# Two transformer blocks on one core: the three post-norms, the norms behind them and the output worked in halves of the tokens

## The chip, the cores and the metric

One core of a Trainium2 chip runs the whole program in one launch. The metric is the device time of an execution in microseconds (us). The core has a matrix engine (PE, which multiplies a stationary 128x128 tile with a moving one and writes PSUM), a vector engine (DVE), an activation engine (ACT), a general engine (POOL), and SyncE (SP), which issues the DMAs here. Each engine runs its own list of instructions in the order written; they wait for each other on semaphores.

## The reference

512 tokens with 1024 channels go through two blocks, all in float32. The first is a gated mixer (a depthwise convolution, a gated delta rule with 8 heads in both directions), a gated feed-forward part, a gated per-layer input and a last norm. The second is a feed-forward part, a mixer (pooled windows and window attention with sinks), and a feed-forward part again; each of its three parts has a norm before and a norm after it. What bears on the change:

```python
def rms_norm(x, g):
    return x * lax.rsqrt(jnp.mean(x * x, axis=-1, keepdims=True) + NORM_EPS) * g

x = x + jax.nn.sigmoid(rms_norm(x, g_pl[i]) @ w_pl_gate[i]) * pl
x = rms_norm(x, g_final)

h = swiglu(rms_norm_2(x, ffn1_pre[l]), ffn1_w_gu[l], ffn1_w_down[l])
x = x + 0.5 * rms_norm_2(h, ffn1_post[l])
h = token_mixer(rms_norm_2(x, mix_pre[l]), ...)
x = x + rms_norm_2(h, mix_post[l])
h = swiglu(rms_norm_2(x, ffn2_pre[l]), ffn2_w_gu[l], ffn2_w_down[l])
x = x + 0.5 * rms_norm_2(h, ffn2_post[l])
```

Every norm takes the mean square over all 1024 channels of a token. Different tokens don't meet in it.

## The kernel before, in words

**Layout.** Activations lie with channels on the 128 partitions: `x` is 8 tiles of 128 channels by 512 tokens. A **unit** is one weight block of 128 output channels, loaded by SP into one of four slots `w_raw`. Each float32 operand is split into a high and a low part (`w_hi` by ACT at L1020, `w_lo` by DVE at L1446; `a_hi` by ACT at L1295, `a_lo` by DVE at L1471), so a unit of a projection from 1024 channels is 8 x 3 = 24 products of 128x512 at L571 (`products`). A down projection of a feed-forward part has 22 channel tiles, two units (66 products) for one output tile. All go to the two banks of `pg`, in turns; an `Outs` table names who evacuates each. `gemm` counts finished units, and `hi`/`lo` of unit n + 2 wait for unit n (`after`).

**Order of the work.** It is written out by hand, one list an engine. The stages of this study, by unit names: `pg` 0 to 7 (gate of the per-layer input), `fg1`/`fu1` and `fd1` (first feed-forward part of block two), `mk`, `mv`, `mq`, `mu` (mixer), `mo` 0 to 7 (its output), `fg2`/`fu2`, `fd2`, and then the output.

**A norm** (`square`, `adds`, `norm`, `root`, `recip`, `norm_out`). ACT squares each tile into one of two buffers `sq`, POOL adds them up in `acc` (L2073), PE sums over channels with one-column products against ones (L602, 16 passes, since a float32 product of PE is two), ACT takes the root (L1042), DVE the reciprocal (L1458), PE spreads it over the partitions (L609, 8 passes), and DVE copies it to `rstd` (L1462). A norm whose result only scales columns of a product is put in late: the next stage's products run on unscaled `x`, and their evacuation multiplies with `rstd`; `norm_out` sits 14 products (`NORM_AT`) into the second unit of that stage.

**The post-norms** can't be put in late, since their result is added to `x`. After `fd1`, `mo` and `fd2` the function `post` scales the kept output (`hb`, `hb2`) by `rstd`: the first four tiles (`PD`) on DVE at L1924, the other four on POOL at L2146. DVE adds each to `x` (L1928), ACT makes `a_hi` and the square of the new `x`, and DVE `a_lo`. After `pg` the last norm of block one takes its place: DVE multiplies `x` with gain and `rstd` (L1909). The first unit of the next stage waits for `a_lo`, tile by tile. After `fd2` SP stores each of the 8 tiles of `x`.

## Time and profile before

| what | us |
|---|---|
| median of 3 runs | 2404.41 |
| lowest, highest | 2402.77, 2405.77 |
| the profiled execution | 2404.79 |
| its span | 2402.9 |
| PE busy | 2230.9 |
| DVE busy | 1304.9 |
| ACT busy | 788.9 |
| POOL busy | 327.7 |

The span runs from the first to the last event of the core in the profile. Busy time of PE counts overlapping, pipelined products once, with ends that are modelled, so it doesn't say that PE works at its peak. The time of a stage is best read from starts of products. Numbers in the timeline are microseconds from the start of the span.

### The profile page before, as it was taken

What the parts mean: (1) busy time and instruction counts of PE and PEld (TensorE: products, weight loads), DVE (VectorE), ACT (ScalarE), POOL (GpSimd) and SP (SyncE); (2) the same over time, 40 slices, a digit from 0 to 9 for tenths busy, and PEclk for the clock granted to TensorE, in tenths of its full rate; (3) what the DMA queues carried; (4) which work ended last, traced back from release to release, by engine and by line L of the source; (5) the groups of instructions that cost most, each with busy time, mean ns of one, the idle gap of its engine ahead of it and who ended that gap; (6) DMA issues with size and microseconds to landing.
All of it is one profiled execution on the core that took longest, in us unless ns stands there. A gap on an engine that the chain in (4) does not pass through costs nothing.

```text
span 2402.9 us, 33875 instructions
## 1 busy us (share of the span) xinstructions
PE 2230.9 (93%) x13850; PEld 1832.4 (76%) x13850; DVE 1304.9 (54%) x1750; ACT 788.9 (33%) x1106; POOL 327.7 (14%) x228
## 2 busy tenths in 40 slices
PE   6999888899899999999999979999988897999996
PEld 4877777778787878888888768888876575888885
DVE  4578798887654446444443354444226835444423
ACT  4345222225433223333322333332223443323221
POOL 0100442130343310100000120000011212000001
PEclk8999899999899999999999979999997986999998
DMA  3232011112111123322232312223221111222321
GB/s 139 82 115 79 28 54 41 45 50 79 36 41 41 54 71 137 122 96 96 96 108 93 105 53 96 96 96 108 96 85 44 36 59 45 97 96 96 111 94 40
DMA packets 54901, 189.68 MB, mean 79 GB/s; under 512 B 6144, under 2 KB 6400, under 8 KB 54784
## 3 DMA queue, kind: packets, MB, share of 16 engines
q1 hardware_dynamic: 51904, 182.75, 22.6%
q10 hardware_dynamic: 2880, 5.24, 0.6%
q8 instruction: 89, 1.46, 0.3%
q14 instruction: 28, 0.23, 0.0%
HBM read 178.53 MB, written 9.44 MB: 78 GB/s over the span
## 4 chain that ended last, share of the span: by engine, by line
PE 77%; DVE 13%; issue 6%; ACT 2%; DMA 1%; SPq 0%; POOL 0%; DVEq 0%; ACTq 0%; POOLq 0%
PE pg L571 65%; PE pC L746 3%; PE pB L602 2%; DVE cpad L1490 2%; DVE w_lo L1446 1%; DVE x L1928 1%; DVE a_lo L1471 1%; PE pB L746 1%; PE pC L609 1%; PE pB L609 1%; DVE oT L1490 1%; DVE sacc L1600 1%; DVE cacc L1490 1%; ACT w_hi L1020 1%; DVE hb L1924 1%
## 5 line engine op out<-in xcount | busy, mean ns | idle before, releaser
L571 PE MATMUL pg<-a_hi,w_hi 128*128 128x512 f32 x1904 | 770.6, 405 | 49.5 <-DVE a_lo L1471 36.2
L571 PE MATMUL pg<-a_hi,w_lo 128*128 128x512 f32 x1904 | 763.8, 401 | 0.0
L571 PE MATMUL pg<-a_lo,w_hi 128*128 128x512 f32 x1904 | 761.9, 400 | 0.0
L1446 DVE TENSOR_TENSOR w_lo<-w_raw,w_hi 128x1024 fp32r<-128x1024 f32 (+3 forms) x299 | 389.1, 1301 | 458.8 <-ACT w_hi L1020 458.7
L1020 ACT ACTIVATE w_hi<-w_raw 128x1024 fp32r<-128x1024 f32 (+3 forms) x299 | 329.6, 1102 | 669.1 <-PE pg L571 648.0
L571 PEld LDWEIGHTS pg<-a_hi,w_hi 128*128 128x128 f32 x1904 | 366.5, 192 | 142.3 <-issue 31.4
L571 PEld LDWEIGHTS pg<-a_hi,w_lo 128*128 128x128 f32 x1904 | 366.6, 193 | 78.4 <-issue 1.3
L571 PEld LDWEIGHTS pg<-a_lo,w_hi 128*128 128x128 f32 x1904 | 367.1, 193 | 74.2 <-issue 0.7
L2073 POOL TENSOR_TENSOR acc<-acc,sq 128x512 f32<-128x512 f32 x64 | 95.1, 1486 | 1368.3 <-ACT sq L1037 1367.4
L571 PE MATMUL pg<-h_hi,w_hi 128*128 128x512 f32 x528 | 208.0, 394 | 0.0
L571 PE MATMUL pg<-h_hi,w_lo 128*128 128x512 f32 x528 | 207.0, 392 | 0.0
L571 PE MATMUL pg<-h_lo,w_hi 128*128 128x512 f32 x528 | 204.9, 388 | 0.0
L1847 DVE TENSOR_TENSOR tmp<-pg,rstd 128x512 f32<-128x512 f32 x66 | 45.7, 692 | 189.3 <-PE pg L571 189.3
L2090 POOL TENSOR_TENSOR ls<-lc,consts 128x512 f32<-128x512 f32 x48 | 74.6, 1561 | 461.5 <-ACT lc L1247 452.9
L571 PEld LDWEIGHTS pg<-h_hi,w_lo 128*128 128x128 f32 x528 | 99.1, 188 | 23.2
L571 PEld LDWEIGHTS pg<-h_lo,w_hi 128*128 128x128 f32 x528 | 99.1, 188 | 22.2
L571 PEld LDWEIGHTS pg<-h_hi,w_hi 128*128 128x128 f32 x528 | 99.3, 188 | 19.7
L1490 DVE SCALAR_TENSOR_TENSOR cpad<-cpad,vec 128x512 f32<-128x512 f32 x120 | 102.0, 911 | 0.2
L1252 ACT ACTIVATE yb<-pC 128x512 f32<-128x512 f32 x40 | 24.0, 599 | 188.1 <-PE pC L746 188.1
L1318 ACT ACTIVATE h_hi<-tmp 128x512 f32 (+1 forms) x66 | 41.7, 632 | 131.7 <-DVE tmp L1851 131.7
L1600 DVE SCALAR_TENSOR_TENSOR sacc<-pad,swt,sacc 128x512 f32<-128x512 f32 x96 | 76.5, 797 | 3.4
L1856 DVE TENSOR_TENSOR h_lo<-tmp,h_hi 128x512 f32 (+1 forms) x66 | 45.7, 692 | 58.3 <-ACT h_hi L1318 58.3
(323 smaller groups left out, 2379.0 us busy)
## 6 DMA issues: line engine op xcount, KB each, us to landing
w_raw<-in_w_gu SPq DMA_DIRECT2D x132, 512.0 KB, 3.3
w_raw<-in_w_in SPq DMA_DIRECT2D x74, 512.0 KB, 3.3
w_raw<-in_w_dn SPq DMA_DIRECT2D x48, 704.0 KB, 4.0
spill_g<-tmp ACTq DMA_DIRECT2D x16, 256.0 KB, 2.0
w_raw<-in_w_co SPq DMA_DIRECT2D x8, 512.0 KB, 3.6
w_raw<-in_w_do SPq DMA_DIRECT2D x8, 512.0 KB, 3.8
w_raw<-in_w_wo SPq DMA_DIRECT2D x8, 512.0 KB, 4.1
w_raw<-in_w_pg SPq DMA_DIRECT2D x8, 512.0 KB, 6.8
```

The costliest lines, as they stand in the source:

```text
L571: ins = pe.matmul(dst, w_of(w, n % 2, k), b(k), start=first and q == 0, stop=last and q == len(todo) - 1)
L602: ins = pe.matmul(dst[:, c:c + 1], src[:, c * P:(c + 1) * P], ones[:, 0:1], start=q == 0, stop=q == len(srcs) - 1)
L609: ins = pe.matmul(dst[:, c * P:(c + 1) * P], factors[:, c:c + 1].to_broadcast([P, P]), ident, start=True, stop=True)
L746: ins = pe.matmul(dst[s, j, :], lhs[s, j, :], id64[s, :] if rhs is None else rhs[s, j, :], start=True, stop=True)
L1020: act.activation(w_hi[:, n % 2, 0:c], w_raw[:, n % 4, 0:c], ACT.Copy).then_inc(S("w_hi"), 1)
L1446: dve.tensor_tensor(w_lo[:, n % 2, 0:c], w_raw[:, n % 4, 0:c], w_hi[:, n % 2, 0:c].bitcast(F32), ALU.subtract).then_inc(S("w_lo"), 1)
L1490: ins = dve.scalar_tensor_tensor(y, src, w, y, ALU.mult, ALU.add)
L1600: ins = dve.scalar_tensor_tensor(y, src, w, y, ALU.mult, ALU.add)
L1847: dve.tensor_tensor(tmp2[:], bu, rstd[:], ALU.mult).then_inc(S("evD"), 1)
L1856: dve.tensor_tensor(at_m(h_lo), tmp2[:], at_m(h_hi).bitcast(F32), ALU.subtract)\
L2073: pool.tensor_tensor(acc[:], acc[:], sq[:, t % 2, :], ALU.add).then_inc(S("add"), 1)
L2090: pool.tensor_tensor(ls[:, lv % 2].rearrange("p (d h) c -> p d h c", d=2), lc[:].rearrange("p (d h) c -> p d h c", d=2), mask, ALU.mult)\
```

## The change

The 512 tokens are split in halves (`TOK`), in four places (`EVENTS`): the end of `pg`, of `fd1`, of `mo` and of `fd2`.

- **Last units of a stage.** The last two of `pg` and `mo` (`late_units`) and the last output of `fd1` and `fd2` (`down`) are multiplied for tokens 0 to 255 first, then for 256 to 511, as products of 128x256. The second half goes to another bank of `pg` under a name with "late". The sums and the spread of the first half's norm (`half_sums`, `half_out`) stand between products of the second half.
- **The norm.** Tiles before the last one or two (`FULL`) are squared and added as before, by `full_square` and `full_adds`; the squares of the rest stay in `sq` and go into PE's sums directly.
- **New `x`.** `new_x` on DVE does a half of a tile at a time: scale straight from PSUM (`nbh`, no copy to `rstd`), new `x`, `a_lo` one and two tiles behind. Steps of other work stand in between by a small table. POOL takes no part. ACT's `new_a` makes `a_hi` and the square.
- **First two units of the next stage** (`early_units`): unit one for the first half of the tokens, tile by tile; unit two for the first half; unit one for the second half, tile by tile; unit two for the second half, with the spread of the norm 14 products in.
- **The norm of the new `x`.** POOL's adds and the sums at their end are replaced: PE sums each half tile's squares as they come (`x_sums`, L682, four passes a half tile), and `x_root` takes the roots.
- **The output** is stored in 16 pieces of half a tile.

```diff
--- before.py
+++ after.py
+        NORMS = [KT] * 4 + [0, 0] + [PT_] * 2 + [0]
...
+        EVENTS = ["pg", "fd1", "mo", "fd2"]
+        FULL = [KT - 2, KT - 1, KT - 2, KT - 1]
...
+        TOK = (slice(0, T // 2), slice(T // 2, T))
+        CH = ((0, 1), (2, 3))
...
-                sp.wait_ge(S("xu"), 2 * KT + t + 1)
-                sp.dma_start(out[t], x[:, t]).then_inc(S("out"), 16)
-            sp.wait_ge(S("out"), 16 * KT)
+            for h in range(2):
+                for t in range(KT):
+                    sp.wait_ge(S("xu"), 6 * KT + KT * h + t + 1)
+                    sp.dma_start(out[t][:, TOK[h]], x[:, t, TOK[h]]).then_inc(S("out"), 16)
+            sp.wait_ge(S("out"), 2 * 16 * KT)
...
-                    ins = pe.matmul(dst, w_of(w, n % 2, k), b(k), start=first and q == 0,
+                    ins = pe.matmul(dst[:, cols], w_of(w, n % 2, k), b(k)[:, cols], start=first and q == 0,
...
+            def half_sums(p, h):
+                pe.wait_ge(S("add"), HA[p] + FULL[p] - 1)
+                pe.wait_ge(S("hq"), HQ[p] + FULL[p] + (KT - FULL[p]) * (h + 1))
+                srcs = [acc[:]] + [sq[:, t % 2, :] for t in range(FULL[p], KT)]
+                for c in CH[h]:
+                    for q, src in enumerate(srcs):
+                        ins = pe.matmul(nbh[h][:, c:c + 1], src[:, c * P:(c + 1) * P], ones[:, 0:1], start=q == 0,
+                                        stop=q == len(srcs) - 1)
+                ins.then_inc(S("nsum"), 1)
+            def half_out(p, h):
+                pe.wait_ge(S("recip"), turn_of(p, h))
+                for c in CH[h]:
+                    ins = pe.matmul(nbh[h][:, c * P:(c + 1) * P], nst[:, 1, NC + c:NC + c + 1].to_broadcast([P, P]),
+                                    ident, start=True, stop=True)
+                ins.then_inc(S("nout"), 1)
+            def x_sums(p, h, t):
+                pe.wait_ge(S("b_hi"), 2 * (2 * KT * p + KT * h + t + 1))
+                for c in CH[h]:
+                    ins = pe.matmul(xss[h][:, c % 2, 0:1], sq[:, t % 2, c * P:(c + 1) * P], ones[:, 0:1],
+                                    start=t == 0, stop=t == KT - 1)
+                ins.then_inc(S("xs"), 1)
+            def late_units(p, keys, sums, outs):
+                ns = [U.at[key] for key in keys]
+                for key, n in zip(keys, ns):
+                    pe.wait_ge(S("w_lo"), n + 1)
+                    begin(key)
+                    products(n, act_a(), KT, bank(key), w_tile, cols=TOK[0]).then_inc(S("half"), 1)
+                for i, (key, n) in enumerate(zip(keys, ns)):
+                    begin(key + ("late",))
+                    q = 0
+                    for at_, todo in sorted([(sums, half_sums), (outs, half_out)], key=lambda z: z[0]):
+                        if i * UNIT <= at_ < (i + 1) * UNIT:
+                            if at_ - i * UNIT > q:
+                                products(n, act_a(), KT, bank(key + ("late",)), w_tile, (q, at_ - i * UNIT), cols=TOK[1])
+                            q = at_ - i * UNIT
+                            todo(p, 0)
+                    products(n, act_a(), KT, bank(key + ("late",)), w_tile, (q, UNIT), cols=TOK[1])\
+                        .then_inc(S("gemm"), 1)
+            def early_units(p, keys):
+                n0, n1 = (U.at[key] for key in keys)
+                pe.wait_ge(S("w_lo"), n0 + 1)
+                begin(keys[0])
+                for t in range(KT):
+                    if t == 5:
+                        half_sums(p, 1)
+                    if t == 7:
+                        half_out(p, 1)
+                    x_sums(p, 0, t)
+                    pe.wait_ge(S("b_lo"), 2 * KT * p + t + 1)
+                    products(n0, act_a(), KT, bank(keys[0]), w_tile, (3 * t, 3 * t + 3), cols=TOK[0])
+                pe.wait_ge(S("w_lo"), n1 + 1)
+                begin(keys[1])
+                products(n1, act_a(), KT, bank(keys[1]), w_tile, cols=TOK[0])
+                for t in range(KT):
+                    x_sums(p, 1, t)
+                    pe.wait_ge(S("b_lo"), 2 * KT * p + KT + t + 1)
+                    ins = products(n0, act_a(), KT, bank(keys[0]), w_tile, (3 * t, 3 * t + 3), cols=TOK[1])
+                ins.then_inc(S("gemm"), 1)
+                products(n1, act_a(), KT, bank(keys[1]), w_tile, (0, NORM_AT), cols=TOK[1])
+                norm_out(PRE[p], na)
+                products(n1, act_a(), KT, bank(keys[1]), w_tile, (NORM_AT, UNIT), cols=TOK[1]).then_inc(S("gemm"), 1)
...
+                def down(q, part, cols, first, last):
+                    return products(U.at[("fd" + f, 2 * KT - 2 + q)], ((lambda k: h_hi[:, KH * q + k, :]),
+                                                                      (lambda k: h_lo[:, KH * q + k, :])),
+                                    KH, dst, w_tile, part, first, last, None, cols)
+                for q in range(2):
+                    pe.wait_ge(S("w_lo"), U.at[("fd" + f, 2 * KT - 2 + q)] + 1)
+                    ins = down(q, None, TOK[0], q == 0, q == 1)
+                ins.then_inc(S("half"), 1)
+                dst = begin(("fd" + f, "late"))
+                down(0, (0, 10), TOK[1], True, False)
+                half_sums(p, 0)
+                down(0, (10, 24), TOK[1], True, False)
+                half_out(p, 0)
+                down(0, (24, 3 * KH), TOK[1], True, False).then_inc(S("gemm"), 1)
+                down(1, None, TOK[1], False, True).then_inc(S("gemm"), 1)
...
-            norm(4)
-            norm_out(4)
-            ffn("1", 5, "ffn1")
-            norm(6)
-            norm_out(6)
...
+            late_units(0, [("pg", KT - 2), ("pg", KT - 1)], UNIT + 6, 2 * UNIT - 1)
+            ffn("1", 4, None)
...
-            unit(("mk", 0), ready=fresh("mix"))
-            norm(7)
-            unit(("mv", 0), part=(0, NORM_AT))
-            norm_out(7)
-            unit(("mv", 0), part=(NORM_AT, UNIT))
+            early_units(1, [("mk", 0), ("mv", 0)])
...
+            late_units(2, [("mo", KT - 2), ("mo", KT - 1)], 9, 22)
+            ffn("2", 8, None)
+            half_sums(3, 1)
+            half_out(3, 1)
...
+            def half_square(p, t, h, src):
+                act.wait_ge(S("add"), HA[p] + t - 2)
+                act.activation(sq[:, t % 2, TOK[h]], src[:, TOK[h]], ACT.Square).then_inc(S("hq"), 1)
+            def new_a(p, h, t, g):
+                act.wait_ge(S("xu"), 2 * KT * p + KT * h + t + 1)
+                act.activation(a_hi[:, t, TOK[h]], x[:, t, TOK[h]], ACT.Copy, scale=v(g, t)).then_inc(S("b_hi"), 1)
+                wait(act, "xs", 2 * KT * p + KT * h + t - 1)
+                act.activation(sq[:, t % 2, TOK[h]], x[:, t, TOK[h]], ACT.Square).then_inc(S("b_hi"), 1)
...
+                act.activation(nst[:, 0, 0:NC], eps_t[:, 0:NC], ACT.Sqrt)
+                def taken(h, key):
+                    half_square(p, m, h, bank(key))
+                    act.activation(hb[:, m, TOK[h]], bank(key)[:, TOK[h]], ACT.Copy, scale=v(g, m))\
+                        .then_inc(S("evA"), 1)
+                act.wait_ge(S("half"), HF[p] + 1)
+                taken(0, ("fd" + f, m))
+                half_root(p, 0)
+                after(("fd" + f, 2 * m))
+                for t in range(KT):
+                    if s:
+                        new_a(p, 0, t, g2)
+                    if t == 3:
                         unit_out(act, ("fd" + f, 2 * m + 1))
-                        square(nu2, m, bank(("fd" + f, m)))
-                        act.activation(hb[:, m], bank(("fd" + f, m)), ACT.Copy, scale=v(g, m)).then_inc(S("evA"), 1)
+                        taken(1, ("fd" + f, "late"))
                         after(("fd" + f, 2 * m + 1))
+                    if t == 5:
+                        half_root(p, 1)
+                if s:
+                    for t in range(KT):
+                        new_a(p, 1, t, g2)
+                    x_root(p)
...
+            def new_x(p, src, factor, g2, between):
+                for h in range(2):
+                    dve.wait_ge(S("nout"), turn_of(p, h))
+                    for i in range(KT + 2):
+                        if i < KT and p:
+                            y = src[:, i, TOK[h]]
+                            dve.tensor_tensor(y, y, nbh[h][:, TOK[h]], ALU.mult).then_inc(S("xt"), 1)
+                        t = i - 1
+                        if 0 <= t < KT:
+                            y = x[:, t, TOK[h]]
+                            if p:
+                                dve.wait_ge(S("xt"), 2 * KT * (p - 1) + KT * h + t + 1)
+                                ins = dve.scalar_tensor_tensor(y, src[:, t, TOK[h]], factor, y, ALU.mult, ALU.add)
+                            else:
+                                ins = dve.scalar_tensor_tensor(y, y, v("g_final", t), nbh[h][:, TOK[h]], ALU.mult, ALU.mult)
+                            ins.then_inc(S("xu"), 1)
+                        t = i - 2
+                        if 0 <= t < KT and g2:
+                            dve.wait_ge(S("b_hi"), 2 * (2 * KT * p + KT * h + t) + 1)
+                            dve.scalar_tensor_tensor(a_lo[:, t, TOK[h]], x[:, t, TOK[h]], v(g2, t),
+                                                     a_hi[:, t, TOK[h]].bitcast(F32), ALU.mult, ALU.subtract)\
+                                .then_inc(S("b_lo"), 1)
+                        for todo in between.get((h, i), ()):
+                            todo()
...
+            gate_in(KT - 1, ("pg", KT - 1, "late"), TOK[1])
+            new_x(0, None, None, "ffn1_pre", {
+                (0, 2): [lambda: gate_out(KT + 1, KT - 1, TOK[1])],
+                (0, 5): [lambda: after(("pg", KT - 1))],
+                (0, 8): [lambda: half_recip(0, 1)]})
+            ffn("1", 4, None)
+            def post_down(f, src, g2):
+                p = EVENTS.index("fd" + f)
+                half_recip(p, 0)
+                new_x(p, src, 0.5, g2, {
+                    (0, 2): [lambda: after(("fd" + f, 2 * KT - 2))],
+                    (0, 5): [lambda: after(("fd" + f, 2 * KT - 1))],
+                    (0, 7): [lambda: half_recip(p, 1)]})
+            post_down("1", hb, "mix_pre")
...
-            def post(nu, k, src):
-                pool.wait_ge(S("rstd"), nu + 1)
-                for t in range(PD, KT):
-                    pool.tensor_tensor(src[:, t], src[:, t], rstd[:], ALU.mult).then_inc(S("xp"), 1)
...
+            def full_adds(p):
+                for t in range(1, FULL[p]):
+                    pool.wait_ge(S("hq"), HQ[p] + t + 1)
+                    wait(pool, "add", HA[p] + t - 1)
+                    pool.tensor_tensor(acc[:], acc[:], sq[:, t % 2, :], ALU.add).then_inc(S("add"), 1)
```

**The order of instructions.** DVE behind `fd1`, before (`hb` is the kept output, `rstd` the norm's factor):

```order
L1458 RECIPROCAL nst<-nst 128x4
L1462 COPY rstd<-pB 128x512
L1924 TENSOR_TENSOR hb<-hb,rstd 128x512
L1928 SCALAR_TENSOR_TENSOR x<-hb,x 128x512
L1924 TENSOR_TENSOR hb<-hb,rstd 128x512
L1928 SCALAR_TENSOR_TENSOR x<-hb,x 128x512
L1471 SCALAR_TENSOR_TENSOR a_lo<-x,vec,a_hi 128x512
L1924 TENSOR_TENSOR hb<-hb,rstd 128x512
L1928 SCALAR_TENSOR_TENSOR x<-hb,x 128x512
L1471 SCALAR_TENSOR_TENSOR a_lo<-x,vec,a_hi 128x512
L1924 TENSOR_TENSOR hb<-hb,rstd 128x512
```

and in the changed kernel, the same place (`pB` holds the factor in PSUM):

```order
L1687 RECIPROCAL nst<-nst 128x2
L1696 TENSOR_TENSOR hb<-hb,pB 128x256 x2
L1702 SCALAR_TENSOR_TENSOR x<-hb,x 128x256
L1696 TENSOR_TENSOR hb<-hb,pB 128x256
L1702 SCALAR_TENSOR_TENSOR x<-hb,x 128x256
L1709 SCALAR_TENSOR_TENSOR a_lo<-x,vec,a_hi 128x256
L1664 TENSOR_TENSOR w_lo<-w_raw,w_hi 128x1024
L1696 TENSOR_TENSOR hb<-hb,pB 128x256
L1702 SCALAR_TENSOR_TENSOR x<-hb,x 128x256
L1709 SCALAR_TENSOR_TENSOR a_lo<-x,vec,a_hi 128x256
L1696 TENSOR_TENSOR hb<-hb,pB 128x256
```

The copy to `rstd` is gone, steps are 256 wide, and a `w_lo` of the next stage, which before stood ahead of the reciprocal, stands between the third and the fourth tile.

PE where `fd1` ends and `mk` begins, before (`h` is the hidden activation, `a` the new set):

```order
L571 MATMUL pg<-h_hi,w_lo 128x512
L602 MATMUL pB<-consts,acc 128x1
L602 MATMUL pB<-consts,sq 128x1
L602 MATMUL pB<-consts,acc 128x1
L602 MATMUL pB<-consts,sq 128x1
L602 MATMUL pB<-consts,acc 128x1
L602 MATMUL pB<-consts,sq 128x1
L602 MATMUL pB<-consts,acc 128x1
L602 MATMUL pB<-consts,sq 128x1
L609 MATMUL pB<-consts,nst 128x128 x4
L571 MATMUL pg<-a_hi,w_hi 128x512
L571 MATMUL pg<-a_lo,w_hi 128x512
```

and in the changed kernel:

```order
L604 MATMUL pg<-h_hi,w_hi 128x256
L604 MATMUL pg<-h_lo,w_hi 128x256
L604 MATMUL pg<-h_hi,w_lo 128x256
L682 MATMUL pA<-consts,sq 128x1 x2
L604 MATMUL pg<-a_hi,w_hi 128x256
L604 MATMUL pg<-a_lo,w_hi 128x256
L604 MATMUL pg<-a_hi,w_lo 128x256
L682 MATMUL pA<-consts,sq 128x1 x2
L604 MATMUL pg<-a_hi,w_hi 128x256
L604 MATMUL pg<-a_lo,w_hi 128x256
L604 MATMUL pg<-a_hi,w_lo 128x256
L682 MATMUL pA<-consts,sq 128x1 x2
```

The sums and the spread of the post-norm no longer stand between the last product and the first of the next stage; the first half's stand earlier, among products of 256 columns, and new sums (L682) stand ahead of every three products.

## Rows read from the trace of the kernel before

**Rows 1.** Page, parts 1 and 2: busy time by engine; granted clock in 40 slices
```profile
PE 2230.9 (93%) x13850; PEld 1832.4 (76%) x13850; DVE 1304.9 (54%) x1750; ACT 788.9 (33%) x1106; POOL 327.7 (14%) x228
...
PEclk8999899999899999999999979999997986999998
```

**Rows 2.** Source line L571, what its engine waited for: us, times
```profile
  DVE a_lo L1471: 64.4, 36
```

**Rows 3.** Windows: length, busy PE, PEld, DVE, ACT, POOL, PEclk, DMA share, GB/s
```profile
46.00:50.00 4.00, 2.58 (x9) 1.16 (x7) 4.00 (x7) 1.27 (x3) 0.00 (x0) 1.00 0.01 4
1404.00:1437.00 33.00, 24.41 (x71) 18.33 (x71) 19.27 (x20) 12.96 (x21) 9.29 (x6) 0.50 0.10 32
1804.00:1830.00 26.00, 19.99 (x51) 13.96 (x52) 18.70 (x23) 8.77 (x14) 9.10 (x6) 0.50 0.06 21
1991.00:2029.00 38.00, 23.65 (x66) 17.08 (x67) 25.68 (x25) 12.53 (x19) 16.17 (x10) 0.51 0.08 28
```

**Rows 4.** Timeline of PE behind `fd1`: start, us, engine, line, operation
```profile
1790.34 0.40 PE L571 MATMUL pg<-h_hi,w_lo 128*128 128x512 f32 x1
...
1833.92 0.39 PE L571 MATMUL pg<-a_hi,w_lo 128*128 128x512 f32 x1
```

**Rows 5.** Timeline of PE behind `pg`, `mo` and `fd2`
```profile
1399.18 0.39 PE L571 MATMUL pg<-a_hi,w_lo 128*128 128x512 f32 x1
...
1440.99 0.39 PE L571 MATMUL pg<-a_hi,w_lo 128*128 128x512 f32 x1
...
1987.31 0.39 PE L571 MATMUL pg<-a_hi,w_lo 128*128 128x512 f32 x1
...
2031.61 0.39 PE L571 MATMUL pg<-a_hi,w_lo 128*128 128x512 f32 x1
...
2380.96 0.40 PE L571 MATMUL pg<-h_hi,w_lo 128*128 128x512 f32 x1
```

**Rows 6.** Chain, two narrow pieces of PE: start, us, what, passes
```profile
204.02 1.78 PE pC L609 x16
...
541.56 1.68 PE pB L602 x16
```

**Rows 7.** Timeline of DVE and POOL behind `fd1`
```profile
1795.93 0.69 DVE L1462 COPY rstd<-pB 128x512 f32<-128x512 f32 x1 [1.25 <-PE pB L609]
...
1796.70 6.79 POOL L2146 TENSOR_TENSOR hb<-hb,rstd 128x512 f32<-128x512 f32 x4 [19.07 <-DVE rstd L1462]
...
1805.75 0.69 DVE L1928 SCALAR_TENSOR_TENSOR x<-hb,x 128x512 f32<-128x512 f32 x1
...
1806.36 0.74 DVE L1471 SCALAR_TENSOR_TENSOR a_lo<-x,vec,a_hi 128x512 fp32r<-128x512 f32 x1
...
1807.02 0.68 DVE L1924 TENSOR_TENSOR hb<-hb,rstd 128x512 f32<-128x512 f32 x1
...
1808.35 1.77 DVE L1471 SCALAR_TENSOR_TENSOR a_lo<-x,vec,a_hi 128x512 fp32r<-128x512 f32 x1
...
1818.69 1.62 DVE L1471 SCALAR_TENSOR_TENSOR a_lo<-x,vec,a_hi 128x512 fp32r<-128x512 f32 x2
```

**Rows 8.** Groups by form: busy us, mean ns of one, idle before
```profile
L1995 DVE TENSOR_TENSOR sm<-pA,c 128x256 f32<-128x256 f32 x4 | 1.7, 421 | 0.1
...
L1399 ACT ACTIVATE ptb<-pB 128x256 f32<-128x256 f32 x4 | 1.4, 359 | 0.0
...
L1042 ACT ACT_TABLE_LOAD x7 | 9.0, 1283 | 3.1 <-PE pB L602 3.0
...
L1020 ACT ACTIVATE w_hi<-w_raw 128x1024 fp32r<-128x1024 f32 x246 | 260.4, 1059 | 513.6 <-PE pg L571 502.4 <-DMA w_raw<-in_w_pg 6.5 <-PE pg L653 4.5
```

**Rows 9.** Timeline of PE and window behind a wait of the attention stage
```profile
1870.68 0.55 PE L966 MATMUL pB<-consts,sm 128*128 128x128 f32 x3 [2.38 <-DVE sm L2015]
...
1870.00:1875.00 5.00, 4.32 (x19) 3.30 (x20) 3.68 (x11) 1.79 (x7) 0.00 (x0) 0.66 0.33 105
```

**Rows 10.** DMA issues of the end: KB each, us from issue to landing
```profile
out<-x SPq DMA_DIRECT2D x8, 256.0 KB, 2.1
```

302 lines of the change are left out of this document (194 added, 108 removed).

## The prediction

> **What bounds the kernel now.** The page comes first: PE is busy 93% of the span and nobody else comes near, but the line of the granted clock has dips besides the rows of 9 [rows 1]. The list of what line L571 (all big products) waited for says where PE is not fed: 64.4 us in 36 waits behind `a_lo` at L1471, the low half of a new activation set [rows 2]. These waits lie where a stage ends in a norm over all 1024 channels, so that the next stage can't start. The table of busy time by stretch shows the same three places at half the clock: 0.50 of full speed, 1.2 instead of 2.4 GHz [rows 3].
>
> PE's own timeline prices a place. After `fd1` the last product starts at 1790.34; at one step of 0.23 more (call this end X) nothing big remains. The second unit of the next stage starts its last product at 1833.92 [rows 4], so X to its end is 43.6 us, for 48 products that need 48 x 0.228 = 10.9. After `pg` it is 1399.41 to 1441.22, 41.8; after `mo` 1987.54 to 2031.84, 44.3; and after the last product of all (2381.2) 21.7 us pass to the end of the span [rows 5]. That is 118.7 us outside the three pairs of units, 30.9 + 32.7 + 33.4 + 21.7; the change is about this.
>
> **The change, part by part.** I follow `fd1`, from T0, where the last output's first half (tokens 0 to 255) is done. Before, T0 would lie 33 full products ahead of X, so X = T0 + 7.5.
>
> *Half-width products.* 744 of them replace 372: 96 in `pg` and `mo` late units each, 132 in each last `fd` output, 96 early ones at each of three starts. The trace has none of this kind. A full one starts every 0.228 us. The nearest row is the 128-wide pass of a spread, which streams two cycles a column and so as many cycles as 256 single ones: 16 passes in 1.78 us, 0.111 each, own weight load included. A pass of one column, nearly only a weight load, takes 0.105 (16 in 1.68) [rows 6]. Bounds: 0.107, the stream alone, and 0.228, no gain from halving. I take 0.1145, half the full step. The Trainium skill ("TensorE: Matmul & The Clock Gate", Back-to-back issue gap) gives 131 ns a product at 512 columns and 81 at 128, so halving the width would save clearly less than half; with its ratio, about 0.75, the step would be 0.17 and the 744 cost some 42 us more. The trace disagrees on the wide one (228, not 131), so I price this as a rival only.
>
> *First statistic.* Before, the four steps after X (sums, root, reciprocal, spread) end when `rstd` is copied at 1795.93, 5.4 us after X [rows 4, 7]. Now they run under the second half: after 10 products (1.15 us) 8 passes of sums (0.9), root and reciprocal (0.9, hidden by 14 products), 4 passes of spread (0.45); DVE gets the scale at about T0 + 4.35. PE ends the output at T0 + 7.6 + 0.9 + 0.45 = 8.95, which is X + 1.45. The `Sqrt` table load of 1.28 us [rows 8] is asked for ahead of it. Cover gone, these steps would cost 5.4 again.
>
> *DVE.* Before, it made 8 tiles in 24.4 us: the copy at 1795.93, the last `a_lo` done at 1820.3. Steps that take 0.69 alone took 1.6 to 1.8 while POOL ran `hb`, 6.79 us, and the adds [rows 7]. POOL now has nothing to do there. Two independent 512-wide steps start 0.61 to 0.66 apart [rows 7], and 128x256 takes 0.421 against 0.69, 0.27 less [rows 8]. So a half tile costs 0.33 (scale) + 0.34 (`x`) + 0.39 (`a_lo`) = 1.06; for `pg`, without the first, 0.73. ACT's 128x256 step takes 0.36 [rows 8], a pair 0.72, so it keeps up. 16 half tiles are 17 us alone.
>
> *What is queued in between.* In the first half DVE also makes two `w_lo` (1.22 each) and the second reciprocal; the later `w_lo` waits for ACT, which after tile 3 has to take the late half (another pair, 0.72) and make `w_hi` (1.06 [rows 8]). Followed step by step the `a_lo` of tiles 0 to 3 are ready at T0 + 7.2, 9.4, 10.5, 11.5, that of tile 4 only at 15.0, the last at 18.5. PE needs 3 x 0.1145 + 4 x 0.107 (the new one-column sums, between the 0.105 and 0.111 above) = 0.77 a tile. At full clock PE ends the first half of unit one at 19.4, the same half of unit two at 22.2, unit one at 28.9, unit two with its spread at 32.1: 19 us less than before.
>
> *The clock takes some back.* PE then works 3 x 0.107 of every 1.06 us on real columns, 30%, and the one-column passes barely stream. Around T0 + 12 to 15 it gets nothing for 3 us. In the trace, PE starved like this stayed at 0.50 (1804 to 1830, the last 4.5 us of it dense); it held 1.00 from 46 to 50, with 9 wide products in 4 us (9 x 0.228, half the time) [rows 3]; and after the 2.4 us gap before 1870.68 the stretch 1870 to 1875 has 0.66 [rows 9]. So I count on a fall near T0 + 14 and a return during the 24 dense products of unit two (24 x 0.213 = 5.1 us at half clock, about the dense stretch after which it came back at 1830). At half clock a pass doubles to 0.213, and a tile costs PE 7 x 0.213 = 1.5, above DVE's 1.06. Then: first half done at about 22, unit two's half at 27, DVE held until then since `sq` has two buffers and only PE frees them, second half at 33.8, unit two at 38.3. Last, its spread leaves only 10 half products for the copy to `rstd`, a `w_lo` and the evacuation: 0.9 us of wait. T0 + 39.2 = X + 31.7 against X + 43.6: **11.9 us gained**.
>
> *`mo`.* Same, X = T0 + 10.9 with two late units, second unit done at T0 + 41.9 = X + 31.0 against 44.3: **13.3**. *`pg`.* The gating chain (DVE, ACT, DVE, DVE) and two table loads (sigmoid to root and back, 1.28 each) sit in ACT's queue, but a tile has two DVE steps: X + 31.0 against 41.8: **10.8**. The Trainium skill (same page, HAM oscillation) warns of just this: thin pieces of matmul work with waits between keep falling to the low clock. By that rule nothing would come back before the stage is dense again, the second rival's time.
>
> *The end.* From T0: first half's `x` from 4.35 to 11.7 (8 x 0.68, and the second reciprocal, which waits for PE's 8 passes after the last product), second scale at 12.0, last `x` at 17.8; then one store, 2.1 us from issue to landing [rows 10], and the end of the span: 20.3 = X + 12.8 against 21.7: **8.9**. 16 stores of half the size cost SP nothing that counts.
>
> Sum: 11.9 + 13.3 + 10.8 + 8.9 = 44.9. The profiled execution took 2404.79 us (span 2402.9); the median of the runs shown is 2404.41. Forecast **2360 us**.
>
> **Rivals.** (1) *The clock holds.* PE's gaps are shorter than they were, and 46 to 50 shows it held at half load. Then fd1 gives 18.1, mo 19.1, pg 15.9, the end 8.9: 62, **2343 us**. Against it: 30% is less than half.
> (2) *The clock falls and stays low* over both halves, since 1804 to 1830 stayed low through products and sums. PE at 1.5 a tile both times: fd1 3.6, mo 5.1, pg 4.1, end 8.9: 21.7, **2383 us**.
> (3) *Slower: half-width products don't cost half.* If the weight load of the next product isn't hidden behind 256 columns, each costs up to 0.228. On the path are the 456 late ones and 48 x 3 of the second units: 600 x 0.1135 = 68 us, against 45: **2428 us**. It decides from 0.19 a product on (45 / 600 over 0.1145). The 0.111 of the spread speaks against.
> (4) *No effect*: some wait makes the halves run one after the other with nothing beside them, as a late half held behind an evacuation. I find each evacuation 1 to 3 us early, so little chance: **2404 us**.
>
> **How the numbers follow.** The forecast 0.60, clock holds 0.15, clock stays low 0.17, slower 0.05, no effect 0.03. About 0.2% (5 us) is what a measurement can tell from no change. Forecast, first and second rival lie beyond it: faster 0.92; the fourth falls within it: same 0.03; the third: slower 0.05. The range takes in rivals 1 and 2: 2342 to 2384.
>
> **What would show it.** Starts of half-width products 0.11 to 0.12 apart in `pg`'s late units. DVE steps at `x` near 0.42, none at 1.7. Granted clock down for a few us inside each first half, up again before the stage's dense part. The waits of the products for `a_lo` still there, but under 40 us. After the last product some 11 us instead of 21.7. The forecast is wrong if the late units take over 13 us for `mo`'s pair, if the clock never falls, or if it stays at 0.50 through the second half.

## The result, and the profile after

| | before | changed | forecast |
|---|---|---|---|
| median, us (4 runs each) | 2403.59 | 2366.93 | 2360 |
| lowest to highest | 2398.92 to 2405.77 | 2363.57 to 2373.62 | 2342 to 2384 |
| the profiled execution | 2404.79 | 2364.42 | |
| its span | 2402.9 | 2362.6 | |

The ratio is 0.9865, with a 95% interval of 0.9847 to 0.9883: faster by 1.4% (the medians alone divide to 0.985), 36.7 us between the medians, 40.4 between the profiled executions. The forecast of those was 44.9.

The page of the changed kernel, against [rows 1]: the busy time of PE, the granted clock.

```profile
PE 2235.9 (95%) x14382; PEld 1866.3 (79%) x14382; DVE 1280.5 (54%) x1848; ACT 802.0 (34%) x1177; POOL 274.2 (12%) x196
...
PEclk8999999999899999999999989999999988999999
```

PE's share of the span rises by two points, and the dips of the clock to 6 and 7 are gone. What the big products (now L604) and the new sums (L682) waited for, against [rows 2]; these are the lists of two source lines, us and times:

```profile
  DVE w_lo L1664: 20.4, 14
  DVE a_lo L1719: 17.4, 19
...
  DVE a_lo L1709: 1.3, 2
```
```profile
  ACT sq L1198: 7.4, 7
  DVE w_lo L1664: 2.1, 2
```

The 64.4 us behind `a_lo` are 1.3 at L1709, the new `a_lo`. The wait has partly moved: 9.5 us stand before the sums instead, which come ahead of the products, and the waits for `w_lo` are 22.5 with the sums' 2.1, where they were 14.7.

**The span cut at the same products.** A busy share can't say where the 40 us went; starts of products can. A place begins at the first product that the change does in halves (in the kernel before, the same unit's first) and ends with the first product of the third unit behind it, or with the span. I read these starts off PE's timeline of both kernels:

| stretch | before | changed | measured | forecast |
|---|---|---|---|---|
| up to unit 0 of `pg` | 1348.0 | 1344.2 | -3.8 | 0 |
| `pg` units 0 to 5 | 40.5 | 39.1 | -1.4 | 0 |
| `pg` 6 to third unit of the next stage | 52.7 | 47.0 | -5.7 | -10.8 |
| feed-forward one, up to its last output | 334.2 | 334.3 | 0.1 | 0 |
| last output of `fd1` to the third unit | 58.7 | 45.4 | -13.3 | -11.9 |
| mixer, up to `mo` 6 | 142.5 | 144.2 | +1.7 | 0 |
| `mo` 6 to the third unit | 55.2 | 45.8 | -9.4 | -13.3 |
| feed-forward two | 334.2 | 334.3 | 0.1 | 0 |
| last output of `fd2` to the end | 36.8 | 28.3 | -8.5 | -8.9 |

The four places give 36.9 us, 8.0 less than forecast. The other 3.4 come from stretches whose work the change leaves alone. They are chance: over all the profiled executions of this study "up to unit 0" lies between 1344.2 and 1351.9 with no edit there, and the mixer between 141.0 and 145.8 in those without an edit at its end. The granted clock goes with it. In units 0 to 5 of `pg` a stretch of 39.0 to 39.3 us has 1.00, one of 40.5 to 40.8 has 0.96 (e11_width, which edits them, left out); before and changed:

```profile
1348.04:1388.53 40.49, 37.42 (x170) 30.81 (x168) 19.59 (x25) 16.32 (x21) 6.14 (x4) 0.96 0.46 159
```
```profile
1344.23:1383.28 39.05, 35.85 (x169) 29.48 (x168) 19.50 (x25) 16.29 (x21) 6.15 (x4) 1.00 0.48 163
```

The mixer took 141.0 us at 0.94 (e1_statistic) and 145.8 at 0.91 (e3_end). This is also why medians of four runs differ by some us, and why the experiments below are read by their stretches. Where no edit touched a place, its stretch repeated within 1.5 us: 47.0, 47.3, 45.8 (`pg`), 45.4, 45.5, 45.7, 44.6 (`fd1`), 45.8, 45.0, 45.1, 45.0 (`mo`), 28.3 to 28.8 (end, nine times). The last value of each of the first three lists is e11_width's, which had less time at the low clock in `pg` and `fd1`.

The windows of the three starts, before and then changed (us, busy PE, PEld, DVE, ACT, POOL, granted clock, DMA share, GB/s):

```profile
1388.53:1441.22 52.69, 40.49 (x145) 31.54 (x144) 30.28 (x34) 21.14 (x31) 12.36 (x8) 0.68 0.15 49
1775.46:1834.15 58.69, 42.49 (x164) 32.56 (x163) 32.31 (x34) 18.42 (x27) 17.47 (x11) 0.71 0.13 45
1976.65:2031.84 55.19, 39.45 (x146) 30.17 (x144) 30.63 (x29) 19.80 (x30) 18.78 (x12) 0.66 0.13 45
```
```profile
1383.28:1430.28 47.00, 43.15 (x298) 42.30 (x296) 26.93 (x57) 26.83 (x55) 1.54 (x1) 0.82 0.15 47
1764.61:1809.99 45.38, 43.04 (x325) 42.36 (x324) 25.94 (x63) 22.01 (x49) 1.29 (x1) 0.89 0.15 49
1954.15:1999.94 45.79, 42.76 (x298) 42.09 (x296) 24.28 (x58) 22.69 (x52) 1.30 (x1) 0.81 0.14 45
```

The clock column is the time's mean over a stretch that has only two levels, so it gives the time at the low one (1.2 GHz, half of 2.4): (1 - 0.82) / 0.5 x 47.0 = 16.9 us behind `pg`, and 10.0 and 17.4 behind `fd1` and `mo`, where before it was 33.7, 34.0 and 37.5. It still falls and comes back at all three. `fd1`, the one place of the three that gained more than forecast, has the least of it. The windows inside:

```profile
1401.00:1417.00 16.00, 15.57 (x73) 15.45 (x73) 9.01 (x22) 9.05 (x23) 0.00 (x0) 0.50 0.10 34
1786.50:1796.50 10.00, 9.39 (x43) 9.31 (x44) 5.78 (x17) 3.15 (x9) 0.00 (x0) 0.50 0.28 96
1971.00:1987.00 16.00, 14.95 (x71) 14.86 (x71) 9.47 (x26) 6.08 (x17) 0.00 (x0) 0.50 0.18 61
1800.00:1805.60 5.60, 5.60 (x51) 5.60 (x50) 4.67 (x13) 4.31 (x13) 0.00 (x0) 1.00 0.00 0
```

In the low windows PE counts as busy nearly all the time: it is the slow one, and DVE, busy 59% at most, waits for it. The last row is the second half of the tokens behind `fd1`, at full clock with the same tile work.

PE around the fall behind `fd1` and `mo` (timeline, start, us, tile):

```profile
1785.19 0.29 PE L604 MATMUL pg<-a_hi,w_lo 128*128 128x256 f32 x1
1786.49 1.01 PE L682 MATMUL pA<-consts,sq 128*128 128x1 f32 x4 [1.01 <-ACT sq L1198]
1788.11 0.58 PE L604 MATMUL pg<-a_hi,w_hi 128*128 128x256 f32 x1 [0.60 <-DVE a_lo L1709]
```
```profile
1968.17 0.28 PE L604 MATMUL pg<-a_hi,w_lo 128*128 128x256 f32 x1
1969.42 0.61 PE L682 MATMUL pA<-consts,sq 128*128 128x1 f32 x4 [0.97 <-DVE w_lo L1664]
...
1970.69 0.45 PE L604 MATMUL pg<-a_hi,w_hi 128*128 128x256 f32 x1
1970.94 0.42 PE L604 MATMUL pg<-a_lo,w_hi 128*128 128x256 f32 x1
```

Behind `fd1` four tiles pass at full clock and the fall comes with the wait at tile 4. Behind `mo` PE stands already ahead of the first tile, and the second tile is at half clock (0.42 instead of 0.28 a product). Then DVE (timeline), which makes the next `x`:

```profile
1975.00 0.41 DVE L1702 SCALAR_TENSOR_TENSOR x<-hb,x 128x256 f32<-128x256 f32 x1
...
1979.54 0.16 DVE L1687 RECIPROCAL nst<-nst 128x2 f32<-128x2 f32 x1
...
1983.71 0.75 DVE L1696 TENSOR_TENSOR hb<-hb,pB 128x256 f32<-128x256 f32 x2 [2.63 <-PE pB L674]
```

It stands 3.72 us after the first of these rows, since `a_hi` of tile 5 comes behind the root of the second half in ACT's queue, and that root waits for sums that PE makes late, at half clock; 2.63 us more go to the spread.

### The profile page after: what moved, and what is told of

Same layout as the page of the kernel before. It is cut to its first block, busy times and chain, and to the rows that moved or that the text cites. A ratio compares the mean times of both kernels' runs of the same rounds, so it can differ in the third digit from the quotient of the medians.

```text
span 2362.6 us, 35062 instructions
## 1 busy us (share of the span) xinstructions
PE 2235.9 (95%) x14382; PEld 1866.3 (79%) x14382; DVE 1280.5 (54%) x1848; ACT 802.0 (34%) x1177; POOL 274.2 (12%) x196
## 4 chain that ended last, share of the span: by engine, by line
PE 79%; DVE 11%; issue 6%; ACT 3%; DMA 1%; SPq 0%; POOL 0%; DVEq 0%; ACTq 0%; POOLq 0%
PE pg L604 66%; PE pC L850 3%; DVE w_lo L1664 2%; DVE cpad L1740 1%; PE pB L635 1%; ACT w_hi L1143 1%; PE pB L850 1%; PE pC L642 1%; DVE sacc L1850 1%; DVE cacc L1740 1%; DVE oT L1740 1%; PE pA L682 1%; PE pB L666 0%; DMA w_raw<-in_w_pg 0%; PE pA L921 0%
## 5 line engine op out<-in xcount | busy, mean ns | idle before, releaser
L604 PE MATMUL pg<-a_hi,w_hi 128*128 128x512 f32 (+1 forms) x1984 | 782.4, 394 | 16.9 <-DVE a_lo L1719 10.7
L604 PE MATMUL pg<-a_hi,w_lo 128*128 128x512 f32 (+1 forms) x1984 | 773.4, 390 | 0.0
L604 PE MATMUL pg<-a_lo,w_hi 128*128 128x512 f32 (+1 forms) x1984 | 771.6, 389 | 0.0
L604 PEld LDWEIGHTS pg<-a_hi,w_hi 128*128 128x128 f32 x1984 | 381.6, 192 | 95.5 <-issue 12.7
L604 PEld LDWEIGHTS pg<-a_hi,w_lo 128*128 128x128 f32 x1984 | 380.8, 192 | 73.5 <-issue 1.2
L604 PEld LDWEIGHTS pg<-a_lo,w_hi 128*128 128x128 f32 x1984 | 381.2, 192 | 70.7 <-issue 0.7
L604 PE MATMUL pg<-h_hi,w_hi 128*128 128x512 f32 (+1 forms) x572 | 215.7, 377 | 0.6 <-DVE w_lo L1664 0.6
L604 PE MATMUL pg<-h_hi,w_lo 128*128 128x512 f32 (+1 forms) x572 | 214.3, 375 | 0.0
L604 PE MATMUL pg<-h_lo,w_hi 128*128 128x512 f32 (+1 forms) x572 | 212.6, 372 | 0.0
L2418 POOL TENSOR_TENSOR acc<-acc,sq 128x512 f32<-128x512 f32 x22 | 29.7, 1352 | 825.0 <-ACT sq L1186 825.0
L604 PEld LDWEIGHTS pg<-h_hi,w_lo 128*128 128x128 f32 x572 | 107.3, 188 | 21.3
L604 PEld LDWEIGHTS pg<-h_lo,w_hi 128*128 128x128 f32 x572 | 107.4, 188 | 20.4
L604 PEld LDWEIGHTS pg<-h_hi,w_hi 128*128 128x128 f32 x572 | 107.5, 188 | 19.2 <-DVE w_lo L1664 1.0
L2344 POOL TENSOR_TENSOR acc<-acc,sq 128x512 f32<-128x512 f32 x22 | 34.1, 1548 | 561.9 <-ACT sq L1160 561.6
```

The lines of the kernel that those rows point to most:

```text
L604: ins = pe.matmul(dst[:, cols], w_of(w, n % 2, k), b(k)[:, cols], start=first and q == 0, stop=last and q == len(todo) - 1)
L2344: pool.tensor_tensor(acc[:], acc[:], sq[:, t % 2, :], ALU.add).then_inc(S("add"), 1)
L2418: pool.tensor_tensor(acc[:], acc[:], sq[:, t % 2, :], ALU.add).then_inc(S("add"), 1)
```

## The experiments

Each was compared with the kernel before on the same chip. The stretches of the profiled executions (us; in brackets the time at the low clock):

| kernel | `pg` | `fd1` | `mo` | end | median | ratio, 95% |
|---|---|---|---|---|---|---|
| the change | 47.0 (17) | 45.4 (10) | 45.8 (17) | 28.3 | 2366.93 | 0.985 to 0.988 |
| e1_statistic | 47.1 (17) | 44.5 (10) | 43.6 (14) | 28.3 | 2362.92 | 0.981 to 0.985 |
| e2_fill | 41.9 (0) | 42.9 (0) | 45.3 (10) | 28.3 | 2357.77 | 0.978 to 0.983 |
| e3_end | 47.3 (17) | 45.5 (10) | 45.0 (14) | 32.5 | 2372.18 | 0.984 to 0.989 |
| e4_nosums | 43.0 (14) | 43.1 (7) | 43.6 (14) | 28.3 | 2359.93 | 0.981 to 0.985 |
| e5_both | 44.0 (7) | 43.7 (3) | 39.5 (0) | 28.4 | 2360.95 | 0.982 to 0.987 |
| e6_pgroot | 46.8 (17) | 45.7 (10) | 45.1 (14) | 28.3 | 2365.15 | 0.983 to 0.986 |
| e7_all | 44.7 (7) | 42.1 (0) | 39.5 (0) | 28.3 | 2358.06 | 0.980 to 0.985 |
| e8_denser | 47.8 (14) | 43.0 (0) | 41.8 (3) | 28.8 | 2362.52 | 0.982 to 0.985 |
| e9_best | 43.6 (7) | 45.1 (7) | 38.6 (0) | 28.1 | 2354.92 | 0.978 to 0.983 |
| e10_weights | 44.4 (14) | 45.0 (10) | 44.5 (14) | 27.8 | 2363.00 | 0.982 to 0.987 |
| e12_again | 41.9 (0) | 42.4 (0) | 40.2 (3) | 27.7 | 2353.51 | 0.976 to 0.980 |
| e11_width (one execution) | 45.8 (14) | 44.6 (7) | 45.0 (14) | 28.3 | 2370.99 | |

**e1_statistic: the second half's statistic earlier.**

```diff
-                    if t == 5:
+                    if t == (3, 4, 3)[p]:
                         half_sums(p, 1)
-                    if t == 7:
+                    if t == (5, 6, 5)[p]:
                         half_out(p, 1)
```

ACT's `half_root` and DVE's `half_recip` move with it.

> Edit: the second half's statistic of the post-norm one or two tiles earlier in the first half of early_units, on PE (sums at t = 3, 4, 3 instead of 5; spread at 5, 6, 5 instead of 7), ACT (root at 3, 4, 3) and DVE (reciprocal behind the fifth tile). Theory A (order): in the changed kernel DVE stands 1.8 us behind fd1 and 3.7 us behind mo for an a_hi that stands behind this root in ACT's queue, and 2.2 and 2.6 us for the spread; PE idles 1.0 us at tile 4 anyway. The wait goes, the second half starts 2 to 4 us earlier at each of three starts, but PE at the half clock paces the first half, so only a part arrives: 3 to 8 us in all, about 2361 us. Theory B (PE paced): PE has the same work at 1.5 us a tile and the half clock; DVE only waits elsewhere: within 1.5 us of 2367. Theory C (the clock decides): a shorter idle at tile 4 keeps the clock up behind fd1, and this place alone gains 4 us or more.

`mo` gained about 1.5 (43.6 against 45.0 to 45.8), `pg` nothing. `fd1` took 44.5, 0.9 less than in the change and as much as in e11_width, which leaves this place alone but had a shorter fall there. So 1.5 to 3 us in all, at the low edge of theory A or under it. DVE's stand of 3.72 in `mo` became 1.28. Theory C is out: the low clock lasts as long as ever behind `fd1` (10 us). So the order cost something in `mo`, but not what was missing.

**e2_fill: PE kept busy.**

```diff
+                def fill(count):
+                    for _ in range(count):
+                        pe.matmul(pC[:, 0, :], ident, ident, start=True, stop=True)
+
+                fill((9, 2, 5)[p])
                 pe.wait_ge(S("w_lo"), n0 + 1)
                 begin(keys[0])
                 for t in range(KT):
+                    fill(1 if t else 0)
+                    if t == (4, 4, 4)[p]:
+                        fill((4, 8, 4)[p])
```

> Edit: filler products on PE (identity by identity, 128 columns float32, into an unused bank, about 0.22 us each): 9, 2, 5 ahead of the first unit of the next stage behind pg, fd1, mo, one ahead of each later tile of the first half, and 4, 8, 4 more ahead of tile 4. The results are not read. Theory A (the clock takes back): with the clock held at full, a tile costs PE 0.81 + 0.22 and DVE's 1.06 paces; each event gains up to 5 us (the forecast's first rival less the forecast, 17 us over three), less where fillers come late: 5 to 15 us faster, granted clock 1.0 through the first halves. Theory B (the chain of DVE and ACT paces, the clock costs little): the same time or up to 3 us slower, with the clock at 1.0 all the same. Theory C (fillers don't hold the clock): it falls all the same, and 8 + 8 + 8 fillers at 0.43 us cost up to 15 us.

The windows of the three stretches in e2_fill:

```profile
1390.05:1431.95 41.90, 40.02 (x337) 39.34 (x336) 26.94 (x57) 26.75 (x55) 1.54 (x1) 1.00 0.17 52
1766.28:1809.17 42.89, 42.18 (x359) 41.68 (x358) 25.88 (x63) 22.13 (x49) 1.30 (x1) 1.00 0.16 52
1951.78:1997.05 45.27, 43.20 (x330) 42.70 (x328) 24.29 (x58) 22.68 (x52) 1.29 (x1) 0.89 0.14 45
```

This run tells most. Behind `pg` PE does 20 products more that nobody reads, 4.4 us of work, and the stretch is 5.1 us shorter; behind `fd1` it is 2.5, both at 1.00 throughout. Behind `mo` the clock fell late, when PE stood at tile 5, and nothing was gained. Theory A: the low clock cost `pg` at least 5.1 us. Theories B and C are out. (The 41.9 us of `pg` are also the forecast's, but the forecast had a low clock in them; more on this below.)

**e3_end: the end without its overlap.**

```diff
+                if p == 3:
+                    down(0, None, TOK[1], True, False).then_inc(S("gemm"), 1)
+                    down(1, None, TOK[1], False, True).then_inc(S("gemm"), 1)
+                    half_sums(p, 0)
+                    half_out(p, 0)
+                    return
```

> Edit: behind fd2 alone the first half's sums and spread stand behind all products, as they would without the overlap; products still in halves. Theory A (the statistic hidden under the second half and the first half's x beside it are what the end gained): DVE starts at X + 2.6 instead of X - 4.7; 16 half tiles of 0.67 and one store follow: the time from the last product to the end of the span is about 15.5 us instead of 10.9, 4.6 us slower in all. Theory B (the end is bound by the stores' queue or the second statistic): less than 2 us slower.

The end took 32.5 instead of 28.3, 4.2 us more (4.6 expected). The first step of DVE, 2.3 us behind the last product:

```profile
2355.11 0.28 PE L604 MATMUL pg<-h_hi,w_lo 128*128 128x256 f32 x1
...
2357.48 0.75 DVE L1702 TENSOR_TENSOR hb<-hb,pB 128x256 f32<-128x256 f32 x2 [0.80 <-PE pB L674]
```

So half of the 8.5 us gained at the end is the overlap of statistic and first half with products. The other 4.3 stay without it, with half tiles on one engine and stores that start as each is done; no run parts these two.

**e4_nosums: the price of the new sums.** The sums of tiles 1 to 7 are left out, so the next norm divides by a root taken over one tile.

```diff
                 for c in CH[h]:
-                    ins = pe.matmul(xss[h][:, c % 2, 0:1], sq[:, t % 2, c * P:(c + 1) * P], ones[:, 0:1],
-                                    start=t == 0, stop=t == KT - 1)
-                ins.then_inc(S("xs"), 1)
+                    if t == 0:
+                        ins = pe.matmul(xss[h][:, c % 2, 0:1], sq[:, t % 2, c * P:(c + 1) * P], ones[:, 0:1],
+                                        start=True, stop=True)
+                if t == 0:
+                    ins.then_inc(S("xs"), 1)
...
```

> Edit: of the one-column sums of the new x (x_sums) those for tiles 1 to 7 of each half are left out, so the norm of the next stage takes the mean square of one tile only; waits and signals stay. It shows what these sums cost PE: 14 half tiles of 4 passes at each of three starts. Theory A (PE paces these starts, at the half clock above all): a tile falls from 1.5 to 0.65 us in the first half, DVE's 1.06 paces, and the second half from 0.81 to 1.06 of DVE; 2 to 5 us a start, 6 to 15 us in all. Theory B (DVE paces them even now): under 3 us in all. The thin work is thinner without them, so the clock should fall at the same place or earlier.

`pg` fell by 4.0, `fd1` by 2.3, `mo` by 1.5 to 2.2: 8 us, theory A. The low clock was shorter too (14, 7, 14 us), so this is the price of the sums where the clock falls, not of their passes alone: against e11_width, whose three places are unedited and had the same time at the low clock (14, 7, 14 us), it is 2.8, 1.5 and 1.4, some 6 us. The last sentence of the expectation didn't come true: the fall behind `mo` came no earlier, 19.9 us into the stretch, against 16.7 in the change and 18.7 in e6_pgroot, where nothing was edited.

**e5_both: e1_statistic and e2_fill.** Fillers at tile 4 are (0, 4, 3).

> Edit: e1_statistic and e2_fill together, fewer fillers ahead of tile 4 (0, 4, 3), since the sums of the second half now stand there or before. In e2_fill the clock held behind pg and fd1 and fell behind mo, where ACT stood 4 us at the root; the stretches were 41.9, 42.9, 45.3 us (changed kernel 47.0, 45.4, 45.8), in e1_statistic 47.1, 44.5, 43.6. Theory A (two separate costs): with the root's wait gone the clock holds behind mo too, and the stretches are about 41.5, 41.5, 41.5, 13 us under the changed kernel's. Theory B (the sums, which stream nearly nothing, take the place of fillers and the clock falls): no better than e2_fill and e1_statistic where it falls.

Theory A came true for `mo` alone, 39.5 us with the clock at 1.00, 6 under the change. Behind `pg` the clock now fell for 7 us, with two of e2_fill's ingredients gone there (4 fillers, and the sums moved ahead). Behind `fd1` it fell for 3.

**e6_pgroot: `pg`'s first statistic earlier.**

```diff
-            late_units(0, [("pg", KT - 2), ("pg", KT - 1)], UNIT + 6, 2 * UNIT - 1)
+            late_units(0, [("pg", KT - 2), ("pg", KT - 1)], UNIT + 6, UNIT + 16)
...
-            gated_late(KT - 2, 1)
+            act.activation(nst[:, 0, 0:NC], eps_t[:, 0:NC], ACT.Sqrt)
             after(("pg", KT - 2))
             half_root(0, 0)
-            gated_late(KT - 1, 1)
+            gated_late(KT - 2, 1)
...
```

On ACT the last `gated_late` follows two tiles later, and DVE's steps in between move with them.

> Edit: behind pg alone, no fillers. In the changed kernel the first new x starts at 0.6 us behind the last product of the stage, behind fd1 4.1 us ahead of it; ACT gates unit 6 late, makes w_hi and loads the table before the root. Here the table is loaded and the root taken first, the late gates follow behind it, the spread stands 16 products into the last unit and not 23. Theory A (the late first statistic is what pg lost against the forecast): first new x about 1.5 to 2 us earlier; the stretch from unit 6 to the third unit falls from 47.0 to about 45. Theory B (the half clock of PE paces the first half): no more than 0.5 us off the stretch. The stretches behind fd1 and mo stay.

The first new `x` came 13.9 us behind the start of unit 6 instead of 15.2, 1.3 earlier, and the stretch gave 0.2. Theory A is out for the changed kernel: with PE at half clock for 17 us, as before, an earlier statistic gives nothing. What it would give with the clock held no run shows. The three stretches:

```profile
1386.87:1433.64 46.77, 43.52 (x297) 42.59 (x296) 26.51 (x57) 27.07 (x56) 1.54 (x1) 0.82 0.15 47
1767.99:1813.64 45.65, 42.90 (x326) 42.23 (x324) 25.95 (x63) 22.00 (x49) 1.29 (x1) 0.89 0.15 49
1959.48:2004.55 45.07, 41.29 (x298) 40.42 (x296) 24.29 (x58) 22.68 (x52) 1.29 (x1) 0.85 0.14 45
```

**e7_all and e8_denser: all together, and more fillers.** e7_all adds e6_pgroot to e5_both, with (4, 2, 5) fillers ahead and (2, 4, 3) at tile 4, and `pg`'s second sums at tile 4 instead of 3. e8_denser is e5_both with (3, 8, 6) at tile 4.

> Edit: e5_both and e6_pgroot together (fillers 4, 2, 5 ahead and 2, 4, 3 at tile 4). If their parts add up, behind pg 41.9 less 1.5 to 2, about 40; behind fd1 and mo as in e5_both.

> Edit: e5_both with 3, 8, 6 fillers ahead of tile 4 instead of 0, 4, 3. Where the clock falls in e5_both and holds here, it is worth 2 us or more a place; where it holds in both, the 3 or 4 further fillers of 0.22 us cost 0 to 0.9 us.

The parts don't add behind `pg` (44.7 and 47.8 instead of 40): in both the clock fell, in e8_denser for 14 us, and PE's passes, fillers among them, then take twice as long. Behind `fd1`, e7_all has e5_both's code word for word and held the clock, 42.1 against 43.7. The 1.6 us between them are about what 3.5 us at half speed lose. e8_denser behind `mo` shows the other side, 41.8 with a short fall and three fillers more.

**e10_weights: the weights of the last unit earlier.**

```diff
             for t in range(KT - 2):
                 unit_out(act, ("mo", t))
+                if t == KT - 3:
+                    after(("mo", t))
                 full_square(2, t, bank(("mo", t)))
                 act.activation(hb2[:, t], bank(("mo", t)), ACT.Copy, scale=v("mix_post", t)).then_inc(S("evA"), 1)
-                after(("mo", t))
+                if t < KT - 3:
+                    after(("mo", t))
```

The same for `pg` (ACT and DVE) and for the second to last output of `fd1` and `fd2`.

> Edit: no fillers; the weights of unit 7 of pg and mo (and of the second unit of the last output) are split into high and low parts ahead of the evacuation work of tile 5 (6) on ACT and DVE. In the changed kernel PE waits 1.17 us for unit 7's low part in pg, 0.60 in mo and 0.31 in each fd, since half-width units leave half the time. Theory A: the waits go and the first statistic comes as much earlier: pg stretch 47.0 to 45.8, mo 45.8 to 45.2, fd1 and end 0.3 each: 2.4 us in all. Theory B (the late stretch isn't what sets the end; PE starts the next unit no earlier since DVE paces it): under 1 us in all.

`pg` 44.4, 2.6 less; `fd1` 0.5, `mo` about 0.8, the end 0.5: 4.4 us, more than theory A's 2.4. Most of the surplus is `pg`'s, and its low clock lasts 14 us, not 17. That difference can be chance: e11_width, with nothing edited from unit 6 on, had 14 us too and took 45.8, and against it `pg` gained 1.4. Read so, with `mo` against 45.0, the weights give some 3 us. In the wait list of the products `w_lo` is back where it was before the change (14.7):

```profile
  DVE a_lo L1727: 21.7, 21
  issue: 17.0, 24
  DVE w_lo L1672: 14.4, 5
```

**e9_best and e12_again: the best of each.** e9_best has e10_weights, the order of e1_statistic behind `fd1` and `mo`, and fillers (9, 2, 5), (4, 6, 3). e12_again takes `pg` from e2_fill as it was and puts 8 fillers at tile 4 behind `fd1`.

> Edit: for each start what did best so far: behind pg the fillers of e2_fill with the second half's sums where the change has them, behind fd1 and mo e5_both's order with 6 and 3 fillers at tile 4; and the weights of e10_weights. Stretches expected if the parts add: pg 41.9 less 1.2 = 40.7, fd1 42.1 less 0.3 = 41.8, mo 39.5 less 0.6 = 38.9, end 28.3 less 0.3: 16.5 us under the changed kernel's profiled execution. Theory B: the clock falls at one of the three, as it did behind fd1 in e5_both and not in e7_all with one and the same code: 3 to 5 us less of that.

> Edit: e9_best, but behind pg exactly what e2_fill had there (its weights' order too), where the clock held for the whole stretch, and behind fd1 8 fillers at tile 4, with which it held in e2_fill and e8_denser. Theory A (the pattern of work sets whether the clock holds): pg 41.9, fd1 42 to 43, mo 38.6, end 28.1, no low clock in the three, the profiled execution 14 to 16 us under the changed kernel's in these stretches. Theory B (the same pattern holds in one execution and falls in another, as fd1's in e7_all and e5_both): at least one of the three shows some us at the low clock and is 2 to 4 us longer.

e9_best: 38.6 behind `mo`, the shortest of all, and falls of 7 us behind `pg` and `fd1`, its theory B. The windows of e12_again:

```profile
1389.98:1431.89 41.91, 40.03 (x337) 39.34 (x336) 26.93 (x57) 26.74 (x55) 1.54 (x1) 1.00 0.16 52
1766.22:1808.64 42.42, 42.01 (x359) 41.70 (x358) 25.94 (x63) 22.16 (x49) 2.25 (x1) 1.00 0.16 53
1949.37:1989.60 40.23, 39.82 (x327) 39.61 (x326) 24.37 (x58) 22.81 (x52) 1.84 (x1) 0.96 0.16 52
```

`pg` repeated e2_fill to 0.01 us (41.91 and 41.90), clock included. `mo`, with e9_best's code, fell for 3 us and took 40.2 instead of 38.6. So both theories have a case. With 0.9779 (0.9760 to 0.9798), 49.1 us under the kernel before, e12_again is the fastest kernel here, 12.4 more than the change gave.

**e11_width: what a narrower product costs** (one execution, 2370.99 us).

```diff
...
+                    for c in range(0, T, P if t == 3 else 2 * P):
+                        ins = products(n, act_a(), KT, bank(("pg", t)), w_tile,
+                                       cols=slice(c, c + (P if t == 3 else 2 * P)))
...
```

> Edit: units 2 and 3 of pg, which the change leaves whole (24 products of 512 columns, 5.44 us each), are done in pieces: unit 2 in two halves (48 products of 256), unit 3 in four quarters (96 of 128). Theory A (a product costs its columns down to 256, and below that what its weight load takes, as the one-column passes at 0.105 us suggest): unit 2 takes 48 x 0.119 = 5.7 us, unit 3 takes 96 x 0.105 = 10.1 us, 4.9 us more for the kernel. Theory B (columns alone count): unit 3 takes 96 x 0.06 = 5.8 us. The third rival of the prediction put the edge at 256 already.

The first products of unit 2 (256 columns), of unit 3 (128), and of unit 4 (512):

```profile
1363.64 0.28 PE L604 MATMUL pg<-a_hi,w_hi 128*128 128x256 f32 x1
...
1369.39 0.22 PE L604 MATMUL pg<-a_hi,w_hi 128*128 128x128 f32 x1
...
1380.07 0.44 PE L604 MATMUL pg<-a_hi,w_hi 128*128 128x512 f32 x1
```

Unit 2 takes 5.75 us, 0.120 a product; unit 3 takes 10.68, 0.111 a product. Theory A, with 0.111 for its 0.105. A whole unit is 5.44.

## Why the prediction was right, and where it was not

The time lies 7 us from the forecast and well inside the range; its likeliest case, a clock that falls in the first half and comes back, is what happened. Part of the closeness is luck. Of the 40.4 us between the profiled executions 3.4 come from stretches with the same code, and two larger errors in the places themselves work against each other: the path at full clock is longer than the steps that were added up, and the low clock seems to cost less than was taken off for it. By its steps:

- **Half-width products**: 0.1145 taken, 0.120 measured with `a` (24 starts of `mo` from 1954.15 to 1956.91) and 0.118 with `h` (33 of `fd1` from 1764.61 to 1768.38). Over 744 that is some 3.5 us that the sum lacks. The third rival is refuted, by e11_width too: 256 columns cost 0.120, far from its 0.228. The trace was right to go by, and not the estimate of 0.75 for a halving that the prediction worked out from the Trainium skill ("TensorE: Matmul & The Clock Gate", Back-to-back issue gap): 48 half products took 5.75 us, 24 whole ones 5.44.
- **First statistic** behind `fd1`: hidden as said. First new `x` at 1777.99, 4.1 ahead of the end of the last product; e3_end priced the same cover at the end, 4.2.
- **DVE**: 1.06 a half tile, measured 1.06 (1782.89, 1783.95 are two starts at `x`); no step of 1.7 is left.
- **The clock takes some back** behind `fd1`: a fall 13.6 us behind the end of the first half (14 said), a return as unit two's dense half begins. The size was too careful: half clock lasted 10 us, not 13, and ended 1.0 us into the dense products, not 5.1 (2.4 in `pg`, 3.1 in `mo`). The forecast took 6.2 us off for it (the first rival's 18.1 less 11.9); e2_fill, whose fillers may themselves cost a little, puts it at 2.5 or somewhat more. Forecast 46.8 for the stretch, 45.4 came.
- **"`mo`. Same"** is the step that failed, and `pg`'s "X + 31.0" with it: `mo` took 45.8 us and `pg` 47.0, where 41.9 were forecast for each. Only `fd1` had been followed tile by tile. From the first halves' end on, `fd1` took 26.3 us to the end of unit two's first half, `mo` 28.5 and `pg` 29.1, where the forecast had 24.2 for `mo`. The fall comes earlier here: with two short late units, PE is through before it is fed. In `mo` it waits 0.97 for a `w_lo` ahead of the first tile, in `pg` 1.84 us. The clock falls at the second tile, and the low clock holds for 17 us instead of 10. It costs 5.1 us in `pg` (41.9 at full clock in e2_fill and e12_again) and 4 to 5 in `mo` (43.6 in e1_statistic with 14 us of it, 39.5 in e5_both). But the forecast had already taken off 5.1 and 5.8 for the clock there (the first rival's gains less its own), so the earlier fall explains the smaller part of the shortfall at most.
- **The path at full clock** is the larger part. With the clock held, `pg` took 41.9 us and not the first rival's 36.8, `fd1` 42.9 and not 40.6, `mo` 39.5 with the root's order mended, some 41 without, and not 36.1: up to 12 us more in all, while the clock cost up to 5 less than forecast. (Both are upper ends, since the fillers stand in these stretches too. Behind `pg`, where PE runs without a gap at most of the tiles, the 11 from tile 1 on are up to 2.4 us of the 41.9; by as much the path would be shorter and the clock's price higher.) Pieces of it that can be read: the waits for `w_lo` in the late units and the wider products (next point), the root in ACT's queue, and the first statistic, whose factor reaches DVE in `mo` 11.2 us behind the start of unit 6 (1965.38), for 5.5 + 4.35 forecast. In `pg` the first new `x` comes at 15.2 us, against 11.9 in `mo`, behind gating steps and two table loads. The forecast named these and set the missing scale step of a tile against them; how much of `pg`'s loss they are is open.
- **The late pair of `mo`**: the prediction called itself wrong if it took over 13 us, and it took 14.1. Of that, 0.76 from start to start is the wait for unit 7's `w_lo`, unforeseen: a half-width unit leaves ACT and DVE half the time to split the next weights. The rest is width and twelve sum passes for eight. e10_weights removes the waits and gains 3 to 4.4 us in all. By its own test the forecast failed here; its time held all the same, since what is missing is small against its range and `fd1` gave 1.4 us more than forecast.
- **ACT's queue**: the root of the second half held up `a_hi` by 3.7 us in `mo` and 4.1 in `pg`; unforeseen, worth 1.5 us in `mo` and nothing in `pg`.
- **The end**: 8.5 for 8.9. From the last product to the end of the span it took 10.9 us. The forecast had 11.3: its 12.8 count from X, and 1.45 of them are still products. The products ahead, a wait of 0.31 for a `w_lo` among them, took 17.5 us instead of 16.5.
- **The second half**, from the end of unit two's first half to the third unit, took 10.8 us at all three places (12.2 forecast), at full clock. The forecast's own full-clock times give 10.8 as well (32.1 and 0.9 less 22.2); the rest was for a DVE held up until then, which behind `fd1` had begun the second half at 1794.71, 4.5 us before.
- **First rival** (the clock holds, 62 us): it did not hold, but its price can now be read. Held, the stretches are 41.9, 42.1 to 43.0 and 38.6 to 39.5; the rival had 36.8, 40.6, 36.1. In sum they lie 14 to 16 us under the change, some 2 to 3 of it from the mended orders, where the rival had 17 for the clock alone. The Trainium skill's warning (same page, HAM oscillation) was right in kind: the clock fell at each start. But in the changed kernel it came back by itself in the first half of unit two, at all three places.

**Open:** one piece of code gave a held clock in one execution and a fall of 3 us in another (`fd1` in e7_all and e5_both, `mo` in e9_best and e12_again); units 0 to 5 of `pg` do the same without any edit. What differs between executions wasn't tried. Fillers help all the same: over the three places the low clock lasts 34 to 44 us in every kernel without them and 3 to 17 in the six with them. The time up to unit 0 of `pg`, which varies by 7.7 us, goes with the time at the low clock too, if loosely: 92 to 96 us of it in the three shortest, 109 and 113 in the two longest. Nor was it tried what halving alone gives: the change also takes POOL out of this work, and DVE's steps of 1.6 to 1.8 us, which it had beside POOL, are gone with it. A kernel with whole tiles and no share for POOL would tell the two apart.

## What to carry to other kernels

Splitting the work at a barrier pays when statistic, elementwise work and products of two halves can run beside each other, and half-width products still cost about half. Follow every such place step by step; a result carried over from the neighbour was 4 and 5 us off here. Look at what PE does in the microseconds before it is fed: behind a wait ahead of thin work the clock was low through most of it, here up to 5 us a place, and some 16 to 20 useless dense products in and behind that wait gave most of them back, though not in every execution. And when units get shorter, whatever prepares the next unit (weights to split, evacuations, roots in one queue) has that much less time: look for waits on it first.

## What the runs showed that was not expected

- With the clock down, a product of 256 columns starts 0.213 after the last, a group of sums and three products of a tile takes 1.5 us instead of 0.81, and DVE ends up waiting for PE.
- 128 columns cost 0.111 a product and 256 cost 0.120: the step hardly changes there, while 512 cost 0.227.
- Useless work made a kernel faster: e2_fill adds 53 fillers, 0.22 us each, about 12 us of PE, and is 9 us faster by the median and 8 in its stretches.
- A stretch at full clock repeats to 0.01 us between two kernels and executions (`pg` in e2_fill and e12_again, `mo` in e5_both and e7_all), while those with a fall vary by up to 1.5.
- The noise of this kernel is in good part the clock's: the same code of `pg` 0 to 5 takes 39 us at 1.00 and 40.5 to 40.8 at 0.96.
